# Where the first norm's root is applied: to x ahead of the in-projection, or to what the in-projection gives

## The chip, the cores and the metric

One core of one Trainium2 chip. The time is the device time of one launch in microseconds (us), median of the runs shown. The engines of the core are TensorE (PE, with its weight loads PEld), VectorE (DVE), ScalarE (ACT), GpSimd (POOL) and SyncE (SP), which here only issues transfers. Each works through its own queue in order and waits on semaphores.

## The reference, cut to what matters

One layer of a streaming encoder over 512 tokens of width 1024: a first norm, an in-projection whose columns feed a forgetting attention, an mLSTM with a causal convolution, and gates, then cross-attention and an MLP. The part at stake:

```python
xf = x.astype(float32)
xn = (xf * rsqrt(mean(xf * xf, -1) + EPS)) * norm_mix
proj = xn @ w_in
fq, fk, fv, ff, mqk, mv, mo, mi, mf, gpre = split(proj)
y_fox = fox_attention(fq, fk, fv, ff + b_fox_f)
qk = silu(causal_conv(mqk, conv_w, conv_b))
hm = mlstm_chunkwise(mq, mk, mv, mi + b_mlstm_i, mf + b_mlstm_f)
y_ml = norm(hm) * mlstm_norm * sigmoid(mo)
g = sigmoid(gpre + b_gate)
merged = g_fox * (y_fox @ w_up_fox) + g_ml * (y_ml @ w_up_mlstm)
```

The root of a token is one number, so it may be applied before the product or after it.

## The kernel before, in words

Every large product is made of three matmuls: both operands are split into a high part, rounded to the fast format, and a low part, and high*high, high*low and low*high are summed in a bank of PSUM. Four token tiles of 128 are turned on PE so that the contraction lies on the partitions.

**Order.** `make_steps` writes out one list of steps, and every engine walks the same list and does its part of each step. Its backbone are the halves (L132): a half is four contraction slabs of 128 for one output group, 12 matmuls of 512 columns (L1504). A unit of 512 output columns has four groups, so eight halves. `before(h, ...)` puts steps ahead of half h and `after(h, ...)` behind it. Behind a half come first the steps called soon (L351), then the weight splits of the second kind and the `take` of a finished group, then the rest, and last the weight splits of the first kind (L371). The units of `w_in` come in the order fox_v (halves 0 to 7), fox_q (8 to 15), fox_k (16 to 23), conv_q, conv_k (24 to 39), ml_v, ml_o (40 to 55), gate_fox0, gate_ml0, gate_fox1 (56 to 79) and, after two products of the up-projection, gate_ml1.

**Weights.** SP loads `stage` in lots of four slabs (1 MB, L690), into two buffers for `w_in`. A lot is loaded when DVE has made the low parts of the lot that held its buffer (L684). A pair of slabs is split by `split_weights`: ACT writes `w_hi` with the norm's gain as scale (L814), DVE writes `w_lo` (L1093). Pairs 4 and 5 are the lot of halves 8, 10, 12 and 14 (lot 2); pairs 8 and 9 (lot 4) take lot 2's buffer, and their splits stand behind half 8. The ring of split slabs holds 12.

**First norm.** For tile n: ACT squares x with a sum (`norm`, L892) and gives the seed of the root (L902); DVE works out the root (L1072 to L1074) and writes `scaled` = x times root in two pieces (L1278); PE turns eight blocks (`norm_turn`, L1548); ACT writes `act_hi` (two copies, L956) and DVE `act_lo` (L1321) (`norm_split`). PE opens with six warm-up matmuls, turns the gains, and makes nine more warm-up matmuls (L1720); each is two records in the trace.

**What takes the groups.** fox_v and ml_v: a copy on ACT. fox_q and fox_k: ACT writes the high part from the bank (L825), DVE the low part from the bank (L1169, L1173). conv_q and conv_k: ACT copies the bank to `conv_u` (L838) and writes `conv_acc` from the bank (L842), and in the same step DVE adds three shifted terms (L1180); tanh and the product follow one and two halves later. ml_o and the gates: a tanh on ACT from the bank (L845, L855). A bank is free for the group after next once it is taken.

**Attention beside it.** From half 23 on each second half is followed by the forgetting attention of one pair of heads and one tile: `pair_scores` on PE (L1602), in `pair_exp` the maxima on DVE (L1367) and two exponentials on ACT (L990), `pair_norm` on DVE (L1375) one half later. `pair_scores` t waits for the exponentials of t-1. From half 60 the mLSTM tasks stand so, one per half: `scores` t on PE (L1646) waits for the weighted product of t-1 on DVE (L1398). `fox_split` p takes a finished pair (ACT L1028, DVE L1403).

Of the kernel before, what the change touches and what calls it, by code (L numbers as in the profile page):

```python
# [38 lines left out]
WARM_UP = (6, 9)  # L39
# [177 lines left out]
def make_steps():  # L217
# [10 lines left out]
    def first(name):  # L228
# [115 lines left out]
    for i, (n, j, c, *_) in enumerate(HALVES):  # L344
        b, a = at.pop(i, ([], []))
        steps += b + [("half", i)]
        if in_products(n):
# [3 lines left out]
        soon = [x for x in a if x[0] in ("pair_exp", "pair_norm", "pair_turned", "probs", "turned", "conv_tanh",  # L351
                                      "conv_silu", "split_weights")]
# [34 lines left out]
    for step, n in steps:  # L387
        spread.append((step, n))
        if step == "norm" and n != 1:
            spread += [("norm_root", n), ("norm_scale", n)]  # L390
# [3 lines left out]
def trunk(nc, x, mem, norm_mix, norm_xattn, norm_mem, norm_mlp, w_in, b_fox_f, b_mlstm_i, b_mlstm_f,  # L394
# [6 lines left out]
    with ExitStack() as ctx:  # L401
# [27 lines left out]
        stat = sb("stat", [P, 2, 8])  # L429
        first_sum, first_mean = sb("first_sum", [P, NT]), sb("first_mean", [P, NT])  # L430
# [37 lines left out]
        dwt = at("dwt", 56, [P, TOK])  # L468
        conv_u = at("conv_u", 58, [P, 2, TOK + 16])
# [51 lines left out]
        s_xroot = sem("s_xroot")  # L521
# [23 lines left out]
        s_qhigh = sem("s_qhigh")  # L545
# [164 lines left out]
        def _(pool):  # L710
# [60 lines left out]

            pool.wait_ge(s_value, X0)
# [12 lines left out]
            pool.wait_ge(s_scaled, 2 * (NT + 2))  # L785
            load_row(row_b, norm_xattn, s_row_b)
            load_row(row_a, norm_mlp, s_row_a)
            pool.wait_ge(s_scaled, 2 * (2 * NT + 2))
# [4 lines left out]
        def _(act):  # L793
# [23 lines left out]
            def take(g):  # L817
# [6 lines left out]
                if k == "fox_q":  # L824
                    act.activation(fq_hi[:, j, :], b[:], ACT.Copy, scale=FOX_HD ** -0.5).then_inc(s_qhigh, 1)  # L825
                elif k == "fox_k":
                    copy(fk_hi[:, j, :], b[:]).then_inc(s_qhigh, 1)
                elif k == "fox_v":
                    copy(fox_v[:, j, :], b[:]).then_inc(free, 1)
                elif k == "ml_v":  # L830
                    copy(ml_v[:, j, :], b[:]).then_inc(free, 1)
                elif k in ("conv_q", "conv_k"):
                    c = j + (4 if k == "conv_k" else 0)
                    if c == 0:
                        act.wait_ge(s_const, N_CONST)
                    if c >= 2:
                        act.wait_ge(s_acc, c - 1)
# [950 lines left out]
```

## Time and profile before

| | us |
|---|---|
| median of 3 runs (935.67 to 935.85) | 935.72 |
| the profiled execution | 935.99 |
| its span on the core | 934.3 |
| TensorE busy | 921.0 |
| VectorE busy | 551.6 |
| ScalarE busy | 427.6 |

The span is what the trace covers; the execution's own time is 1.7 us longer. Matmuls are pipelined: a record of 512 columns is shown as 0.39 us, while the next one starts 0.23 us after it. The page gives the granted clock of PE as a share of full speed, and the column reads 1.00 ahead of its first event.

### The profile page before, as it was taken

The page shows a single profiled execution, that of the slowest core. Times are in us where ns is not written, and L with a number is a line of the kernel's source. Part 1 is how long each engine was busy: PE and PEld are TensorE (multiplying, and loading weights), DVE is VectorE, ACT ScalarE, POOL GpSimd, SP SyncE. Part 2 cuts the span into 40 slices and gives each one's busy share as a digit, 9 for nine tenths or more (in the row PEclk, how much of TensorE's full clock was granted, in tenths as well). Part 3 has the DMA queues.
Part 4 walks back from the last instruction along what each step waited for, and adds up shares of the span by engine and source line. Part 5 has one row for each costly group of instructions (what it writes and reads, how often), then busy time and mean ns, then how long its engine had stood idle before and what let it go on. Part 6 is the DMA issues. An engine that isn't in the chain of part 4 may idle for free.

```text
span 934.3 us, 11910 instructions
## 1 busy us (share of the span) xinstructions
PE 921.0 (99%) x4614; PEld 758.3 (81%) x4614; DVE 551.6 (59%) x997; ACT 427.6 (46%) x744; POOL 15.5 (2%) x40
## 2 busy tenths in 40 slices
PE   7999999999999999999999999999999999999997
PEld 6878778777787888889888778988888888888886
DVE  5534777424557645778143545668847956885543
ACT  5544466534433314345244543376346436534523
POOL 5000000000000000000000000000000000000000
PEclk9999999999999999999999999999999999999999
DMA  7311222122201552344421432120621261062202
GB/s 274 130 35 62 90 91 69 42 71 91 90 1 46 188 173 90 112 136 133 161 91 45 136 135 91 46 90 1 225 91 46 90 226 46 1 226 90 90 1 91
DMA packets 44687, 92.10 MB, mean 99 GB/s; under 512 B 1764, under 2 KB 1864, under 8 KB 44632
## 3 DMA queue, kind: packets, MB, share of 16 engines
q1 hardware_dynamic: 43048, 86.02, 27.3%
q0 software_dynamic: 1568, 5.32, 1.6%
q8 instruction: 37, 0.61, 0.3%
q14 instruction: 18, 0.15, 0.1%
q10 hardware_dynamic: 16, 0.00, 0.0%
HBM read 89.24 MB, written 2.10 MB: 98 GB/s over the span
## 4 chain that ended last, share of the span: by engine, by line
PE 87%; DVE 7%; ACT 4%; issue 1%; ACTq 0%; POOL 0%; DVEq 0%; POOLq 0%
PE bank L1504 64%; PE bank L1535 12%; DVE w_lo L1093 2%; DVE conv_acc L1180 2%; PE bank L1660 1%; PE bank L1709 1%; ACT w_hi L795 1%; PE bank L1548 1%; PE bank L1646 1%; PE bank L1687 1%; PE bank L1674 1%; DVE peak L1367 1%; PE bank L1602 1%; PE bank L1629 1%; PE bank L1614 0%
## 5 line engine op out<-in xcount | busy, mean ns | idle before, releaser
L1504 PE MATMUL bank<-act_hi,w_hi 128*128 128x512 f32 (+1 forms) x640 | 247.7, 387 | 0.1
L1504 PE MATMUL bank<-act_hi,w_lo 128*128 128x512 f32 (+1 forms) x640 | 242.8, 379 | 0.0
L1504 PE MATMUL bank<-act_lo,w_hi 128*128 128x512 f32 (+1 forms) x640 | 242.4, 379 | 0.0
L1089 DVE TENSOR_TENSOR w_lo<-stage,w_hi 128x1024 fp32r<-128x1024 f32 x130 | 153.0, 1220 | 65.0 <-ACT w_hi L795 64.6
L795 ACT ACTIVATE w_hi<-stage 128x1024 fp32r<-128x1024 f32 x130 | 130.3, 1051 | 89.7 <-PE bank L1504 31.7
L1504 PEld LDWEIGHTS bank<-act_hi,w_lo 128*128 128x128 f32 x640 | 120.3, 188 | 23.1
L1504 PEld LDWEIGHTS bank<-act_hi,w_hi 128*128 128x128 f32 x640 | 120.6, 188 | 22.2 <-DVE w_lo L1089 0.6
L1504 PEld LDWEIGHTS bank<-act_lo,w_hi 128*128 128x128 f32 x640 | 120.6, 188 | 21.3
L1504 PE MATMUL bank<-w_hi,act_hi 128*128 128x512 f32 (+1 forms) x264 | 102.9, 390 | 3.8 <-DVE act_lo L1321 2.0
L1504 PE MATMUL bank<-w_hi,act_lo 128*128 128x512 f32 (+1 forms) x264 | 101.2, 383 | 0.0
L1504 PE MATMUL bank<-w_lo,act_hi 128*128 128x512 f32 (+1 forms) x264 | 101.1, 383 | 0.0
L1093 DVE SCALAR_TENSOR_TENSOR w_lo<-stage,gain_col,w_hi 128x512 fp32r<-128x512 f32 x88 | 60.3, 746 | 26.3 <-ACT w_hi L795 26.3
L1504 PEld LDWEIGHTS bank<-w_hi,act_hi 128*128 128x128 f32 x264 | 49.6, 188 | 14.5 <-issue 2.8
L1504 PEld LDWEIGHTS bank<-w_hi,act_lo 128*128 128x128 f32 x264 | 49.6, 188 | 9.8
L795 ACT ACTIVATE w_hi<-stage,gain_col 128x512 fp32r<-128x512 f32 x88 | 56.2, 713 | 2.5 <-PE bank L1504 2.5
L1504 PEld LDWEIGHTS bank<-w_lo,act_hi 128*128 128x128 f32 x264 | 49.7, 188 | 9.4 <-issue 0.2
L1221 DVE TENSOR_TENSOR act_lo<-ff,act_hi 128x512 fp32r<-128x512 f32 (+1 forms) x32 | 18.9, 592 | 60.2 <-ACT act_hi L795 60.0
L865 ACT ACTIVATE ff<-bank 128x512 f32<-128x512 f32 x32 | 19.0, 593 | 49.1 <-PE bank L1504 49.1
L1535 PE MATMUL bank<-w_hi,act_hi 128*128 128x512 f32 x96 | 37.3, 389 | 0.0
L1535 PE MATMUL bank<-w_lo,act_hi 128*128 128x512 f32 x96 | 37.3, 389 | 0.0
L1535 PE MATMUL bank<-w_hi,ff_lo 128*128 128x512 f32 x96 | 37.3, 389 | 0.0
L795 ACT ACTIVATE act_hi<-bank 128x512 fp32r<-128x512 f32 x32 | 17.6, 596 | 35.4 <-PE bank L1548 30.0
(290 smaller groups left out, 1292.9 us busy)
## 6 DMA issues: line engine op xcount, KB each, us to landing
stage<-in_w_in SPq DMA_DIRECT2D x20, 1024.0 KB, 5.0
stage<-in_w_mlp_in SPq DMA_DIRECT2D x16, 1024.0 KB, 5.3
stage<-in_w_mlp_out SPq DMA_DIRECT2D x16, 1024.0 KB, 5.5
stage<-in_w_xkv SPq DMA_DIRECT2D x8, 1024.0 KB, 4.9
stage<-in_w_mix_out SPq DMA_DIRECT2D x4, 1024.0 KB, 4.9
stage<-in_w_xq SPq DMA_DIRECT2D x4, 1024.0 KB, 5.7
stage<-in_w_xo SPq DMA_DIRECT2D x4, 1024.0 KB, 4.9
x_tok<-in_x SPq DMA_DIRECT2D x4, 512.0 KB, 7.3
```

Of the source, the lines that this page charges most:

```text
L795: return act.activation(dst, src, ACT.Copy, **k)
L865: act.activation(ff[:, t, :], b[:], ACT.Relu).then_inc(free, 1)
L1089: dve.tensor_tensor(w_lo[:, r:r + 2, :], stage_pair(pair), w_hi[:, r:r + 2, :].bitcast(F32), ALU.subtract).then_inc(s_low, 1)
L1093: ins = dve.scalar_tensor_tensor(w_lo[:, r + d, :], stage_pair(pair)[:, d, :], gain_of(pair, d), w_hi[:, r + d, :].bitcast(F32), ALU.mult, ...
L1180: ins = dve.scalar_tensor_tensor(acc, u[:, q:q + TOK], conv_taps[:, c, q:q + 1], acc, ALU.mult, ALU.add)
L1221: dve.tensor_tensor(act2_lo[:, t, toks], ff[:, t, toks], act2_hi[:, t, toks].bitcast(F32), ALU.subtract).then_inc(s_al, 1)
L1367: dve.tensor_reduce(peak[:], two[1][:, :, 0:P * (n % NT + 1)], AX_X, ALU.max, negate=True)\
L1504: ins = pe.matmul(dst, still[q], moving[q], start=(k == 0 and q == 0), stop=(k == nk - 1 and q == 2))
L1535: ins = pe.matmul(dst, s, w[:, slab % RING, :], start=(u == 0 and g == 0), stop=(u == 3 and g == 2))
L1548: ins = pe.transpose(bank[2 + 2 * (n % 2) + b][:, P * q:P * q + P], scaled[:, n % 2, P * k:P * k + P], ident[:])
L1602: pe.matmul(bank[2 + d][:, 0:keys], still, moving, start=(q == 0), stop=False)
L1629: ins = pe.matmul(bank[6 + p % 2][r:r + FOX_HD, P * i:P * i + P], fox_v[:, j, col:col + FOX_HD], prob_t[:, d, P * j:P * j + P], start=(j = ...
```

## The change

The roots leave the path of x. PE turns x itself, and the four roots of a tile (`x_root`, one column per token tile) are worked out later. What is laid out by tokens (fox_v, ml_v) gets its root as the scale of ACT's copy. What is laid out by columns needs a row of roots: DVE makes four diagonal matrices from the identity, PE multiplies ones by them into bank 7, and ACT copies the bank to `row_root`; POOL copies that later to `row_root_late`. DVE then multiplies each group of fox_q, fox_k, conv_q, conv_k, ml_o and the gates out of its bank by the row, and ACT works from what DVE wrote. The low parts of fox_q and fox_k and the sums of the convolution become steps of their own, one half later; tanh and product of the convolution move by one half too. The nine warm-up matmuls become one. The order of the first steps changes.

```diff
-WARM_UP = (6, 9)
+WARM_UP = (6, 1)
...
-    steps += [("norm", 0), ("split_weights", 0), ("norm_turn", 0), ("norm_split", 0), ("split_weights", 1),
-              ("split_weights", 2), ("norm", 1), ("split_weights", 3), ("norm_root", 1), ("norm_scale", 1)]
-    after(1, ("norm_turn", 1), ("norm_split", 1), ("norm", 2))
-    after(2, ("norm_turn", 2), ("norm_split", 2), ("norm", 3))
-    after(4, ("norm_turn", 3), ("norm_split", 3), ("split_weights", 4), ("split_weights", 5))
+    steps += [("norm_turn", 0), ("norm_split", 0), ("split_weights", 0), ("split_weights", 1)]
+    before(1, ("norm_turn", 1), ("norm_split", 1), ("split_weights", 2), ("split_weights", 3), ("norm", 0),
+           ("norm_root", 0))
+    before(3, ("norm_turn", 2), ("norm_split", 2), ("norm", 1), ("norm_root", 1))
+    before(5, ("norm_turn", 3), ("norm_split", 3), ("norm", 2), ("norm_root", 2))
+    after(5, ("norm", 3), ("norm_root", 3), ("split_weights", 4), ("split_weights", 5))
+    before(first("fox_q") + 1, ("spread_roots", 0))
+    for p in range(2 * PAIRS):
+        after(group_end(UNIT["fox_q" if p < PAIRS else "fox_k"], p % PAIRS), ("fox_low", p))
...
-        after(g + 1, ("conv_tanh", c))
-        after(g + 2, ("conv_silu", c))
+        after(g + 1, ("conv_sum", c))
+        after(g + 2, ("conv_tanh", c))
+        after(g + 3, ("conv_silu", c))
...
+            pool.wait_ge(s_row_root, 1)
+            pool.wait_ge(s_fturn, N_FOX)
+            pool.tensor_copy(row_root_late[:], row_root[:]).then_inc(s_row_late, 1)
...
                 if k == "fox_q":
-                    act.activation(fq_hi[:, j, :], b[:], ACT.Copy, scale=FOX_HD ** -0.5).then_inc(s_qhigh, 1)
+                    taken(act, g)
+                    copy(fq_hi[:, j, :], fq_scaled[:, j, :]).then_inc(s_qhigh, 1)
...
                 elif k == "fox_v":
-                    copy(fox_v[:, j, :], b[:]).then_inc(free, 1)
+                    act.wait_ge(s_xroot, j + 1)
+                    copy(fox_v[:, j, :], b[:], scale=x_root[:, j:j + 1]).then_inc(free, 1)
...
-                    copy(conv_u[:, c % 2, 3:3 + TOK], b[:]).then_inc(s_conv_u, 1)
+                    taken(act, g)
                     if c >= 2:
                         act.wait_ge(s_silu, c - 1)
                     act.wait_ge(s_prep, 1)
-                    act.activation(conv_acc[:, c % 2, :], b[:], ACT.Identity, scale=conv_taps[:, c, 3:4],
-                                   bias=conv_bias[:, c:c + 1]).then_inc(free, 1)
+                    act.activation(conv_acc[:, c % 2, :], conv_u[:, c % 2, 3:3 + TOK], ACT.Identity,
+                                   scale=conv_taps[:, c, 3:4], bias=conv_bias[:, c:c + 1]).then_inc(s_conv_u, 1)
...
+                elif step == "spread_roots":
+                    act.wait_ge(s_spread, 1)
+                    copy(row_root[:], bank[7][:]).then_inc(s_row_root, 1)
...
                 if k == "fox_q":
-                    dve.wait_ge(s_qhigh, j + 1)
-                    dve.scalar_tensor_tensor(fq_lo[:, j, :], b[:], FOX_HD ** -0.5, fq_hi[:, j, :].bitcast(F32),
-                                             ALU.mult, ALU.subtract).then_inc(free, 1)
+                    group_done(dve, g)
+                    dve.wait_ge(s_row_root, 1)
+                    dve.scalar_tensor_tensor(fq_scaled[:, j, :], b[:], FOX_HD ** -0.5, row_root[:],
+                                             ALU.mult, ALU.mult).then_inc(free, 1)
...
+                    dve.tensor_tensor(conv_u[:, c % 2, 3:3 + TOK], b[:], row_root[:], ALU.mult).then_inc(free, 1)
+                elif k == "ml_o":
+                    group_done(dve, g)
+                    dve.tensor_tensor(ml_th[:, j, :], b[:], row_root[:], ALU.mult).then_inc(free, 1)
+                elif k in ("gate_fox", "gate_ml"):
...
+                    group_done(dve, g)
+                    dve.wait_ge(s_row_late, 1)
+                    dve.tensor_tensor(dst, b[:], row_root_late[:], ALU.mult).then_inc(free, 1)
...
-                if n < NT:
-                    for c in (slice(0, HALF_W), slice(HALF_W, DM)):
-                        dve.tensor_scalar(scaled[:, n % 2, c], x_tok[:, n, c], st[:, 2:3], None, ALU.mult)\
-                           .then_inc(s_scaled, 1)
-                    return
...
+                elif step == "spread_roots":
+                    for i in range(NT):
+                        dve.tensor_scalar(root_diag[:, P * i:P * i + P], ident[:], x_root[:, i:i + 1], None, ALU.mult)\
+                           .then_inc(s_diag, 1)
...
+                if n < NT:
+                    pe.wait_ge(s_xt[n], 16)
...
+                elif step == "spread_roots":
+                    for i in range(NT):
+                        pe.wait_ge(s_diag, i + 1)
+                        ins = pe.matmul(bank[7][:, P * i:P * i + P], ones[:], root_diag[:, P * i:P * i + P],
+                                        start=True, stop=True)
+                    ins.then_inc(s_spread, 1)
```

## Rows read from the trace of the kernel before

**Rows 1.** The page: part 1, busy time; part 4, the chain's shares by engine.

```profile
PE 921.0 (99%) x4614; PEld 758.3 (81%) x4614; DVE 551.6 (59%) x997; ACT 427.6 (46%) x744; POOL 15.5 (2%) x40
...
PE 87%; DVE 7%; ACT 4%; issue 1%; ACTq 0%; POOL 0%; DVEq 0%; POOLq 0%
```

**Rows 2.** Waits of PE: line and releaser, us in total, times, longest us.

```profile
PE bank L1504 <- DVE act_lo L1321: 2.0, 2, 1.0
PE bank L1646 <- DVE ml_den L1398: 2.0, 3, 1.3
PE bank L1504 <- DVE w_lo L1093: 1.8, 2, 0.9
```

**Rows 3.** Windows: length, busy time and instructions of each engine, clock, DMA.

```profile
88.00:162.00 74.00, 74.00 (x451) 58.91 (x449) 53.27 (x94) 45.44 (x98) 0.00 (x0) 1.00 0.23 73
...
223.00:292.00 69.00, 66.90 (x350) 52.76 (x347) 39.73 (x127) 26.92 (x53) 0.00 (x0) 1.00 0.15 47
```

**Rows 4.** Timeline, first 20 us: start, us, engine, line, operation, [idle before <-releaser].

```profile
4.21 1.06 ACT L892 ACTIVATE scaled<-x_tok 128x1024 f32<-128x1024 f32 x1 [1.30 <-DMA x_tok<-in_x]
...
4.71 1.70 PE L1721 MATMUL bank<-ones 128*128 128x128 f32 x7
...
5.46 0.29 ACT L902 ACTIVATE stat<-stat,eps 128x1 f32<-128x1 f32 x1
...
5.66 1.32 ACT L795 ACTIVATE w_hi<-stage,gain_col 128x512 fp32r<-128x512 f32 x2
...
6.63 1.22 PE L1721 MATMUL bank<-ones 128*128 128x128 f32 x7
...
7.42 1.41 DVE L1093 SCALAR_TENSOR_TENSOR w_lo<-stage,gain_col,w_hi 128x512 fp32r<-128x512 f32 x2
...
7.69 1.04 PE L1548 MATMUL bank<-ident,scaled 128*128 128x128 f32 x8
...
8.32 1.08 ACT L795 ACTIVATE act_hi<-bank 128x512 fp32r<-128x512 f32 x2 [1.35 <-PE bank L1548]
8.95 1.29 DVE L1321 TENSOR_TENSOR act_lo<-bank,act_hi 128x512 fp32r<-128x512 f32 x2
...
9.70 0.50 PE L1504 MATMUL bank<-w_hi,act_hi 128*128 128x512 f32 x1 [0.98 <-DVE act_lo L1321]
...
19.63 0.50 PE L1504 MATMUL bank<-w_hi,act_hi 128*128 128x512 f32 x1 [1.02 <-DVE act_lo L1321]
```

**Rows 5.** The chain of waits in order of time, the piece of halves 5 to 9.

```profile
29.86 13.61 PE bank L1504 x60
```

**Rows 6.** Timeline of DVE and ACT, 28 to 94 us.

```profile
28.15 2.74 DVE L1093 SCALAR_TENSOR_TENSOR w_lo<-stage,gain_col,w_hi 128x512 fp32r<-128x512 f32 x4 [0.89 <-ACT w_hi L795]
...
38.56 2.55 ACT L795 ACTIVATE w_hi<-stage,gain_col 128x512 fp32r<-128x512 f32 x4
...
39.92 2.74 DVE L1093 SCALAR_TENSOR_TENSOR w_lo<-stage,gain_col,w_hi 128x512 fp32r<-128x512 f32 x4 [0.40 <-ACT w_hi L795]
...
93.49 0.48 DVE L1375 TENSOR_SCALAR prob<-prob,inv 128x128 f32<-128x128 f32 x2
```

**Rows 7.** The page, part 6: transfers by line, KB each, us from issue to landing.

```profile
stage<-in_w_in SPq DMA_DIRECT2D x20, 1024.0 KB, 5.0
```

**Rows 8.** Timeline of DVE, ACT and PE, 84 to 163 us.

```profile
84.69 0.69 DVE L1173 TENSOR_TENSOR fk_lo<-bank,fk_hi 128x512 fp32r<-128x512 f32 x1 [0.58 <-ACT fk_hi L795]
...
137.47 2.32 DVE L1180 SCALAR_TENSOR_TENSOR conv_acc<-conv_u,param,conv_acc 128x512 f32<-128x512 f32 x3 [1.86 <-ACT conv_acc L842]
139.71 0.68 DVE L1403 TENSOR_TENSOR yf_lo<-bank,yf_hi 128x512 fp32r<-128x512 f32 x1
...
160.38 0.68 DVE L1367 TENSOR_REDUCE peak<-bank 128x2 f32<-128x512 f32 x1
...
161.09 0.47 ACT L990 ACTIVATE prob_b<-bank,peak 128x256 f32<-128x256 f32 x1 [1.27 <-DVE peak L1367]
...
162.17 0.45 PE L1602 MATMUL bank<-fk_hi,fq_hi 64*128 64x384 f32 x2
```

More of the change, by code:

```diff
@@ L388, in make_steps @@
         spread.append((step, n))
-        if step == "norm" and n != 1:
+        if step == "norm" and n >= NT:
             spread += [("norm_root", n), ("norm_scale", n)]
@@ L1171, in take @@
                 elif k == "fox_k":
-                    dve.wait_ge(s_qhigh, PAIRS + j + 1)
-                    dve.tensor_tensor(fk_lo[:, j, :], b[:], fk_hi[:, j, :].bitcast(F32), ALU.subtract)\
-                       .then_inc(free, 1)
+                    group_done(dve, g)
+                    dve.tensor_tensor(fk_scaled[:, j, :], b[:], row_root[:], ALU.mult).then_inc(free, 1)
                 elif k in ("conv_q", "conv_k"):
                     c = j + (4 if k == "conv_k" else 0)
-                    u, acc = conv_u[:, c % 2, :], conv_acc[:, c % 2, :]
@@ L1178, in take @@
-                    taken(dve, g)
-                    for q in range(CONV_K - 1):
-                        ins = dve.scalar_tensor_tensor(acc, u[:, q:q + TOK], conv_taps[:, c, q:q + 1], acc,
-                                                       ALU.mult, ALU.add)
-                        if q < CONV_K - 2:
-                            link(ins)
-                    ins.then_inc(s_acc, 1)
+                    group_done(dve, g)
+                    if c == 0:
+                        dve.wait_ge(s_const, N_CONST)
@@ new lines, in take @@
+                    if c >= 2:
+                        dve.wait_ge(s_acc, c - 1)
+                    dve.tensor_tensor(conv_u[:, c % 2, 3:3 + TOK], b[:], row_root[:], ALU.mult).then_inc(free, 1)
+                elif k == "ml_o":
+                    group_done(dve, g)
+                    dve.tensor_tensor(ml_th[:, j, :], b[:], row_root[:], ALU.mult).then_inc(free, 1)
+                elif k in ("gate_fox", "gate_ml"):
+                    t = 4 * order(n) + j
+                    dst = gate_f[:, t, :] if k == "gate_fox" else gate_m[:, j, :]
+                    if k == "gate_ml" and order(n) == 1:
+                        dve.wait_ge(s_merged, 4)
+                    if k == "gate_ml" and order(n) == 0:
+                        dve.wait_ge(s_silu, 2 * 4)
+                    group_done(dve, g)
+                    dve.wait_ge(s_row_late, 1)
+                    dve.tensor_tensor(dst, b[:], row_root_late[:], ALU.mult).then_inc(free, 1)
@@ L1222, in take, with fox_low, conv_sum @@
                                       ALU.subtract).then_inc(s_al, 1)
+            def fox_low(p):
+                value, high, low = (v[:, p % PAIRS, :] for v in ((fq_scaled, fq_hi, fq_lo) if p < PAIRS else
+                                                                 (fk_scaled, fk_hi, fk_lo)))
+                dve.wait_ge(s_qhigh, p + 1)
+                dve.tensor_tensor(low, value, high.bitcast(F32), ALU.subtract).then_inc(s_qlow, 1)
+            def conv_sum(c):
+                u, acc = conv_u[:, c % 2, :], conv_acc[:, c % 2, :]
+                dve.wait_ge(s_conv_u, c + 1)
+                for q in range(CONV_K - 1):
+                    ins = dve.scalar_tensor_tensor(acc, u[:, q:q + TOK], conv_taps[:, c, q:q + 1], acc,
+                                                   ALU.mult, ALU.add)
+                    if q < CONV_K - 2:
+                        link(ins)
+                ins.then_inc(s_acc, 1)
             def silu(c):
@@ L1335, in _ @@
                     dve.wait_ge(s_gturn, 1)
-                    b16 = bias16[:].unsqueeze(1).to_broadcast([P, NT, 16])
-                    link(dve.tensor_tensor(gate16[:], bank[7][:, 0:16 * NT].rearrange("p (i g) -> p i g", g=16),
-                                           b16, ALU.add))
+                    for i in range(NT):
+                        link(dve.scalar_tensor_tensor(gate16[:, i, :], bank[7][:, 16 * i:16 * i + 16],
+                                                      x_root[:, i:i + 1], bias16[:], ALU.mult, ALU.add))
                     f = gate16[:, :, 0:rows]
@@ L1593, in pair_scores @@
                 if i == 0:
-                    taken(pe, GROUP0[UNIT["fox_k"]] + p)
+                    pe.wait_ge(s_qlow, PAIRS + p + 1)
                 if t >= 1:
```

75 lines of the change are left out of this document (45 added, 30 removed).

## The prediction, made blind

> **What bounds the kernel now.** The page comes first: PE is busy 921.0 of 934.3 us and holds 87% of the chain [rows 1]. So a gain must come from stretches where PE waits, and a loss comes from making it wait. The waits of PE show where those are [rows 2]: twice about 1.0 for `act_lo` and twice 0.9 for `w_lo`, all in the opening, and three waits in the mLSTM stage, 2.0 together. Nothing else holds PE. The windows show how thin its cover is: between 88 and 162 us, convolution beside attention, DVE is busy 53.3 of 74 us, between 223 and 292 us it is busy 39.7 of 69 [rows 3]. The timeline of the opening is what the change rebuilds [rows 4]; the chain piece gives PE's pace, 13.61 / 60 = 0.227 us per matmul, so 2.73 per half, and places half 9 at about 40.6 [rows 5].
>
> **Opening.** Removed: square, seed and roots (ACT 1.06 + 0.29) and two scalings per tile ahead of the turn. x has landed at 4.2, when ACT starts on it. Before, the first turn began at 7.69; now PE is through its gains and one warm-up (two records) at about 4.55 and turns at once, 3.1 us earlier. What then follows, by the new order:
> - Clock. Seven warm-up records from 4.71 take 0.213 each; of the seven from 6.63 to the turn at 7.69 about three take 0.213 and four 0.107 [rows 4]. So PE was at 1.2 GHz until about 7.2 and at 2.4 GHz after it, and the eight turns at 2.4 GHz started about 0.11 apart. At 4.55 they go at the slow pace: four blocks by about 5.6, eight by 6.5.
> - ACT: `act_hi` 5.65 and 6.53 (0.54 each), then w_hi of pair 0 to 8.35, of pair 1 to 9.65. DVE: w_lo of pair 0 (1.41, 1.37 within a run) from 8.4 to 9.8. First matmul at 9.9, against 9.70: the split of pair 0 used to run under the warm-ups and now follows `act_hi` on ACT. Nothing is gained.
> - Pair 1's w_lo ends at 11.1, so half 0 is 12 matmuls in a row, to 12.65 at full clock. Only then comes turn 1, and ACT's w_hi of pairs 2 and 3 stands behind `act_hi` of tile 1, which waits for that turn: `act_hi` 13.35 to 14.4 (0.63 after the turn as in [rows 4]), w_hi 14.4 to 16.95, w_lo from 15.7 to 18.4, half 1's last six matmuls 18.6 to 20.0. Half 2 starts at 20.0 against 19.63: +0.35.
> - The clock was not up when PE fell idle at 6.5. It was up after the warm-ups had run without a gap from 4.12 to 7.2, and half 0 has no such run ahead of it. Bounds: half 0 at 2.4 GHz costs nothing; all 12 matmuls at 1.2 GHz cost 12 x 0.227 = 2.7. I take 2.0, near the slow end, since every record before 7.2 is slow and the rise may fall inside half 0. Opening: +2.35, between -0.5 (turns fast too) and +3.05.
> The Trainium skill, page TensorE: Matmul & The Clock Gate, section Part 4: PE-mode transpose, says that turns don't count as activity for the clock as matmuls do; that speaks against trading warm-ups for turns, and by it the 2.7 is nearer than nothing. The trace before neither bears it out nor denies it, since its turns came after the rise.
>
> **Row of roots, ahead of half 9.** New: four DVE scalings of 128x128 (0.20 to 0.28 each, 0.88 together by the row of two in 0.48 [rows 6]), eight PE records of 0.11 (0.9), an ACT copy of 0.6. On DVE they stand behind the w_lo of pairs 8 and 9, whose splits close the steps of half 8. Before, ACT began these at 38.56 and DVE at 39.92, to 42.66 [rows 6], while PE ran half 9 from 40.6: this was covered, and now PE must wait for it. It also gets later. The splits of pairs 4 and 5 move from behind half 4 to behind half 5, so on ACT behind `act_hi` of tile 3 (29.5 to 30.6) and the square and seed of tile 2 (to 31.9). w_hi runs to 34.45, w_lo ends at 35.95, where it ended at 30.9 [rows 6]. That end lets SP load lot 4. Landing takes 5.0 [rows 7] (4.7 here): 40.65 in place of 35.6. Then w_hi 40.7 to 43.25, w_lo 42.0 to 44.75, diagonals to 45.65, the last two records of PE, half 9 at 45.95. Against 40.6: **+5.35**, of which PE works 0.9. Low bound 0.9 (diagonals in time), high bound with a half run at 1.2 GHz behind the pause: +2.7. Both times move with the opening.
>
> **Multiplications.** 36 on DVE (8 fox, 8 convolution, 4 ml_o, 16 gates), by `fk_lo` 0.69 each or 0.60 in a run [rows 8]: 22 us of DVE, less eight scalings. ACT loses eight copies. fox_q, fox_k: one group per 5.5 us, covered; `fox_low` one half later is long ahead of the scores. A bank is now freed by one DVE instruction, which costs nothing while DVE comes within a group's time. Gates' roots by tile, POOL's copy: covered (DVE idle around 62 us; a half lies between the last pair turn and the first use).
> - Attention, 88 to 162. A convolution tile now needs mult, ACT's `conv_acc`, three sums (2.32 [rows 8]) in two halves, and DVE's maxima queue behind the sums of the step before. I walked the order half by half. First split burst: scores lose about 0.1 at 99.5; second (half 31): exponentials 0.45 late, slack 0.9, covered. At half 35 `yf_lo`, which ran at 139.7 behind the sums [rows 8], comes ahead of them and waits for ACT's `yf_hi` behind exponentials, tanh and `conv_acc`: DVE stands 2.3 us, the maxima of half 37 come 1.5 late (slack 1.1 to the next scores after the ACT part: covered). The lateness doesn't heal before the burst of halves 39 and 40, where two w_lo of 2.74 enclose mult and sums. The maxima at 160.38 come at 162.0, the exponentials end at 163.7 in place of 162.1, and the scores at 162.17 had no slack [rows 8]: +1.6. Together **+1.7**; bounds 0 and 2.9 (all multiplications of the burst uncovered, 1.2 more).
> - mLSTM, 223 to 292. PE's three waits for `ml_den` [rows 2] say that DVE is the last link there. In the steps with a `take` the multiplication stands ahead of the next task's work on DVE, and ACT's tanh then behind it. Where the half's end frees DVE early it runs under PE's values, turns and scores. Three places have no slack: ahead of task 1 (0.6), behind the weight bursts of halves 63/64 (0.7) and 71 (0.9: 0.6 and a tanh ahead of the exponential). **+2.2**, bounds 0 and 2.9.
>
> **Sum.** 2.35 + 5.35 + 1.7 + 2.2 = 11.6. The profiled execution took 935.99 (span 934.3 and 1.7 around it) and would take 947.6; it stood 0.27 above the median, so against the runs: 935.72 + 11.6 = 947.3.
>
> **Rivals.**
> - Faster. The opening's 3.1 us arrive: half 2 starts at 16.5, and the row of roots costs its 0.9 of PE work alone. For it: PE waits 3.8 us there now. Against it: the order of ACT above. Time 935.7 - 3.1 + 0.9 = 933.5. It decides at the first matmul of half 2: later than 19.63 - 0.9 = 18.7 there is no gain left, even with all else covered. 4%.
> - The clock falls in the pauses. PE stands about 3.6 us twice in the opening and over 4 before half 9. If half 9 starts at 1.2 GHz, +2.7, and a second half as much: 950.0 to 952.7. The trace before has no pause over 1.2 us after its rise, so it bears neither. 15%. The Trainium skill, page TensorE: Matmul & The Clock Gate, section HAM oscillation, describes such falls behind waits for data; no run here shows it yet.
> - Lot 4 and the diagonals come in time: the row costs 0.9, time 942.9. 12%.
> - The late maxima and multiplications are covered after all: 947.3 - 3.9 = 943.4. 20%.
> - All parts are covered but the row's 0.9, or they cancel: within 0.2%, which is about what a measurement of this kernel can tell from no change (1.9 us). 4%.
> - The forecast: 45%.
>
> **Numbers.** Slower 0.45 + 0.15 + 0.12 + 0.20 = 0.92, same 0.04, faster 0.04. Range: from the forecast without attention and mLSTM, with a good opening (5.35 - 0.5 = 4.9: 940.6) to the forecast with the high opening and half 9 slow (11.6 + 0.7 + 2.7: 950.7): 940.5 to 951.
>
> **What would show it.** First turn near 4.6 but first matmul near 9.9; w_hi of pair 2 near 14.4 or later; half 2 at 20 to 22; a wait of PE for the diagonals or `w_lo` over 3 us before half 9, with lot 4 landing about 5 us after the w_lo of pair 5; a wait of `pair_scores` of 1 to 2 us once; waits for `ml_den` near 4 us in place of 2.0; a granted clock of 0.5 in the first windows. Wrong if PE reaches half 9 with the diagonals there, or if half 2 starts before 18.7.

## The result, and the profile after

The changed kernel takes **953.09 us** (median of 4 runs, 952.38 to 954.61) beside 935.79 for the kernel before on the same chip (4 runs, 935.67 to 936.3): ratio 1.0186, 95% interval 1.0173 to 1.0199. It is slower, as forecast, but by 17.3 us and not by 11.6; the time lies 2.1 us over the upper end of the range. The profiled execution took 952.66 with a span of 950.3, beside 935.99 and 934.3, so 16.0 of its 16.7 us lie in the span.

The page, parts 1 and 2: busy time, and the granted clock in 40 slices of 23.8 us.

```profile
PE 925.9 (97%) x4606; PEld 761.7 (80%) x4606; DVE 573.0 (60%) x1032; ACT 425.8 (45%) x737; POOL 15.1 (2%) x41
...
PEclk9989999999999999999999999999999999999999
```

DVE's busy time rose by 21.4 against [rows 1], which is about what 36 multiplications and the four diagonals, less eight scalings, should give. PE's rose by 4.9 with eight records fewer: PE had no more to do, it did it more slowly. The waits of PE (line and releaser, us in total, times, longest):

```profile
PE bank L1555 <- DVE w_lo L1111: 6.9, 2, 3.5
PE bank L1786 <- DVE root_diag L1376: 4.9, 1, 4.9
PE bank L1701 <- DVE ml_den L1448: 3.3, 4, 1.3
...
PE bank L1657 <- ACT prob_b L1006: 0.9, 2, 0.7
PE bank L1729 <- ACT prob_t L810: 0.8, 1, 0.8
```

Against [rows 2] there are three long pauses: two of 3.5 for `w_lo`, where the longest wait of the opening was 1.0, and one of 4.9 for the diagonals of the roots. `ml_den` is at 3.3 in place of 2.0. The scores wait 0.7 (`prob_b`), and once the turns of the next weights (`ident`, `prob`) wait 0.8 for ACT's copy of the last ones to `prob_t`, which stands behind a gate's tanh.

Where did the 16.0 us come from? The sharpest view is a subtraction: the start of the first matmul of each half in both traces, and where their difference jumps.

```
half    before    after     later by   step
0         9.70    10.08       0.38    +0.38
1        13.69    19.17       5.47    +5.10
2        19.63    23.17       3.54    -1.93
3        23.28    27.12       3.84    +0.30   opening: 3.84
9        40.59    51.19      10.60    +6.76
10       43.60    55.97      12.37    +1.77   row of roots: 8.53
27      100.54   113.16      12.62    +0.25
43      163.16   176.41      13.25    +0.63   attention: 0.88
61      231.21   245.26      14.06    +0.81
65      247.89   262.27      14.38    +0.33
66      253.19   268.20      15.01    +0.63
73      284.75   300.76      16.00    +0.99   mLSTM: 2.75
last                         16.03
```

**The opening** after, by the timelines of PE, ACT and DVE (start, us, engine, line, operation, [idle before <-releaser]):

```profile
4.72 1.91 PE L1603 MATMUL bank<-ident,x_tok 128*128 128x128 f32 x8
...
7.16 2.55 ACT L810 ACTIVATE w_hi<-stage,gain_col 128x512 fp32r<-128x512 f32 x4
...
8.52 2.74 DVE L1111 SCALAR_TENSOR_TENSOR w_lo<-stage,gain_col,w_hi 128x512 fp32r<-128x512 f32 x4 [0.53 <-ACT w_hi L810]
...
10.08 0.77 PE L1555 MATMUL bank<-w_hi,act_hi 128*128 128x512 f32 x1 [3.45 <-DVE w_lo L1111]
...
14.40 0.39 PE L1555 MATMUL bank<-w_hi,act_lo 128*128 128x512 f32 x1
14.64 1.03 PE L1603 MATMUL bank<-ident,x_tok 128*128 128x128 f32 x8
...
16.24 2.55 ACT L810 ACTIVATE w_hi<-stage,gain_col 128x512 fp32r<-128x512 f32 x4
...
17.61 2.74 DVE L1111 SCALAR_TENSOR_TENSOR w_lo<-stage,gain_col,w_hi 128x512 fp32r<-128x512 f32 x4 [0.42 <-ACT w_hi L810]
...
19.17 0.47 PE L1555 MATMUL bank<-w_hi,act_hi 128*128 128x512 f32 x1 [3.50 <-DVE w_lo L1111]
```

The turn at 4.72 and the first matmul at 10.08 (9.9 forecast) are where the walk of the queues had put them. The first turn's eight blocks take 1.91 where the second's take 1.03, and half 0 takes 4.56, from 10.08 to the next turn at 14.64, where 12 matmuls at 0.227 need 2.73 [rows 5]: it is slow by 1.8. Pair 2's `w_hi`, which waits on ACT for turn 1, starts at 16.24 in place of 14.4, late by as much. The record of the granted clock says the same: it rises at 13.8, is back at half speed from 20.6 to 24.0 and again from 47.9 to 54.7. Windows in and behind those stretches (length, busy time of PE, PEld, DVE, ACT, POOL with counts, clock, DMA share, GB/s):

```profile
20.70:23.90 3.20, 3.20 (x9) 2.55 (x8) 0.32 (x2) 0.49 (x1) 0.00 (x0) 0.50 0.70 209
...
48.00:54.00 6.00, 4.54 (x15) 3.96 (x16) 1.99 (x6) 0.60 (x1) 0.00 (x0) 0.50 0.66 225
56.00:60.00 4.00, 4.00 (x19) 3.31 (x19) 2.02 (x6) 0.63 (x1) 0.00 (x0) 1.00 0.00 0
```

**The row of roots**, the timelines of ACT, DVE and PE from 37 to 56 us:

```profile
45.10 2.56 ACT L810 ACTIVATE w_hi<-stage,gain_col 128x512 fp32r<-128x512 f32 x4 [1.80 <-DMA stage<-in_w_in]
...
37.14 2.74 DVE L1111 SCALAR_TENSOR_TENSOR w_lo<-stage,gain_col,w_hi 128x512 fp32r<-128x512 f32 x4 [0.61 <-ACT w_hi L810]
...
46.47 2.74 DVE L1111 SCALAR_TENSOR_TENSOR w_lo<-stage,gain_col,w_hi 128x512 fp32r<-128x512 f32 x4 [2.12 <-ACT w_hi L810]
49.12 0.87 DVE L1376 TENSOR_SCALAR root_diag<-ident,x_root 128x128 f32<-128x128 f32 x4
...
49.46 2.08 PE L1786 MATMUL bank<-root_diag,ones 128*128 128x128 f32 x8 [4.87 <-DVE root_diag L1376]
51.19 0.77 PE L1555 MATMUL bank<-act_hi,w_hi 128*128 128x512 f32 x1
51.76 0.63 PE L1555 MATMUL bank<-act_lo,w_hi 128*128 128x512 f32 x1
```

Read it as a chain: `w_lo` of pairs 4 and 5 ends at 39.88 and frees the buffer, lot 4 is there at 45.10 (5.2 later; 5.0 in [rows 7]), ACT has waited 1.8 for it, `w_lo` of pairs 8 and 9 ends at 49.1, only then come the four scalings of 0.87 together, and PE has stood 4.9. Its eight records are 1.73 from first start to half 9, in place of 0.9, and half 9 begins with matmuls of 0.43 start to start instead of 0.23.

**Attention and mLSTM**, DVE, ACT and PE (150 to 176 us, then 258 to 260):

```profile
150.38 0.69 DVE L1453 TENSOR_TENSOR yf_lo<-bank,yf_hi 128x512 fp32r<-128x512 f32 x1 [2.23 <-ACT yf_hi L810]
151.84 0.68 DVE L1273 SCALAR_TENSOR_TENSOR ml_k<-conv_th,conv_acc 128x512 f32<-128x512 f32 x1
152.44 2.32 DVE L1263 SCALAR_TENSOR_TENSOR conv_acc<-conv_u,param,conv_acc 128x512 f32<-128x512 f32 x3
154.68 1.22 DVE L1417 TENSOR_REDUCE peak<-bank 128x2 f32<-128x1024 f32 x1
...
161.25 0.42 DVE L1417 TENSOR_REDUCE peak<-bank 128x2 f32<-128x256 f32 x1
164.29 2.74 DVE L1111 SCALAR_TENSOR_TENSOR w_lo<-stage,gain_col,w_hi 128x512 fp32r<-128x512 f32 x4 [2.62 <-ACT w_hi L810]
...
173.63 0.69 DVE L1417 TENSOR_REDUCE peak<-bank 128x2 f32<-128x512 f32 x1
...
175.42 0.44 PE L1657 MATMUL bank<-fk_hi,fq_hi 64*128 64x384 f32 x2 [0.68 <-ACT prob_b L1006]
...
258.45 0.68 DVE L1213 TENSOR_TENSOR gate_f<-bank,row_root_late 128x512 f32<-128x512 f32 x1
259.05 0.41 DVE L1439 TENSOR_REDUCE ml_m<-bank 128x1 f32<-128x256 f32 x1
259.21 0.72 ACT L867 ACTIVATE gate_f<-gate_f,param 128x512 f32<-128x512 f32 x1 [2.23 <-issue]
260.32 0.46 ACT L1022 ACTIVATE dwt<-bank,ml_m 128x256 f32<-128x256 f32 x1
```

DVE does stand 2.2 us for `yf_hi` (2.3 forecast). The maxima that stood at 160.38 [rows 8] stand at 173.63; taking off the 12.62 that PE had already lost, they are 0.63 late, and the scores wait 0.68. In the mLSTM stage the multiplication delays the maximum by 0.60, and the tanh that it lets go on ACT (0.72) stands ahead of the exponential.

### The profile page after: what moved, and what is told of

It reads as the page before. It is cut to its first block, busy times and chain, and to the rows that moved or that the text cites. A ratio compares the mean times of both kernels' runs of the same rounds, so it can differ in the third digit from the quotient of the medians.

```text
span 950.3 us, 11977 instructions
## 1 busy us (share of the span) xinstructions
PE 925.9 (97%) x4606; PEld 761.7 (80%) x4606; DVE 573.0 (60%) x1032; ACT 425.8 (45%) x737; POOL 15.1 (2%) x41
## 4 chain that ended last, share of the span: by engine, by line
PE 69%; DVE 1%; ACT 1%; issue 1%; ACTq 0%; DVEq 0%
PE bank L1555 51%; PE bank L1586 12%; PE bank L1715 1%; PE bank L1764 1%; PE bank L1603 1%; PE bank L1729 1%; PE bank L1742 1%; PE bank L1701 1%; ACT w_hi L810 0%; DVE w_lo L1111 0%; ACT dwt L1022 0%; PE bank L1749 0%; ACT ff L879 0%; DVE w_lo L1107 0%; PE bank L1702 0%
## 5 line engine op out<-in xcount | busy, mean ns | idle before, releaser
L1555 PEld LDWEIGHTS bank<-act_lo,w_hi 128*128 128x128 f32 x640 | 121.0, 189 | 21.4
L1555 PEld LDWEIGHTS bank<-w_hi,act_hi 128*128 128x128 f32 x264 | 50.4, 191 | 17.3 <-issue 7.8
L1555 PEld LDWEIGHTS bank<-w_hi,act_lo 128*128 128x128 f32 x264 | 50.5, 191 | 10.1
```

The costliest lines, as they stand in the source:

```text
L1555: ins = pe.matmul(dst, still[q], moving[q], start=(k == 0 and q == 0), stop=(k == nk - 1 and q == 2))
```

## The experiments

Two theories went in. **A: queues.** The time follows from the order of work on ACT and DVE, the clock adds some 2 us. **B: clock.** The granted clock is low at each of the three pauses and behind it, and that makes up the part that the forecast lacks. Times are medians beside the kernel before in the same batch (935.81 to 936.07). "Later by" is the same subtraction as in the table above.

### Keep PE busy in all three pauses: keep_clock

```diff
+                    for _ in range((9, 15, 0, 0)[n] if n < NT else 0):
+                        pe.matmul(bank[7][:, 0:P], ones[:], ones[:], start=True, stop=True)
                 elif step == "spread_roots":
+                    for _ in range(20):
+                        pe.matmul(bank[7][:, 0:P], ones[:], ones[:], start=True, stop=True)
```

> The changed kernel with idle work for TensorE in its three pauses: 9 products of ones behind the first turn, 15 behind the second, 20 ahead of the row of roots. The queues' order is as changed. If the clock is what my forecast missed, all pauses stay and the granted clock stays at 2.4 GHz from the first half on: about 947.5 us, 5.5 below the changed kernel, and half 9 starts some 5 to 6 us late instead of 6.8 plus 1.8 behind it. Rival (the excess is queueing on VectorE, not the clock): less than 1 us is won, 952 to 953.

Measured 945.95 (945.76 to 946.57), ratio 1.011 [1.0093, 1.0127]: 7.1 below the changed kernel, with work added. The clock is high from 4.8 us until past the last matmul. PE's timeline:

```profile
4.71 1.08 PE L1603 MATMUL bank<-ident,x_tok 128*128 128x128 f32 x8
5.62 2.17 PE L1784 MATMUL bank<-ones 128*128 128x128 f32 x18
...
9.29 0.47 PE L1555 MATMUL bank<-w_hi,act_hi 128*128 128x512 f32 x1 [1.49 <-DVE w_lo L1111]
...
45.12 1.16 PE L1790 MATMUL bank<-root_diag,ones 128*128 128x128 f32 x8 [0.18 <-DVE root_diag L1376]
46.03 0.48 PE L1555 MATMUL bank<-act_hi,w_hi 128*128 128x512 f32 x1
```

The eight turns take 1.08 and not 1.91, the records of the roots 1.16 and not 2.08. The fast turns aren't the edit's doing: the products stand behind them, and the clock rose at 4.8, before the first product. So up to 0.8 us of the gain can be the moment of that rise, which differs between executions (last section). Half 2 starts at 19.48, 0.14 earlier than in the kernel before; between halves 3 and 9 another 5.72 are lost, and 0.11 in half 9; attention costs 0.88 and mLSTM 2.76. This is the change with the clock kept high, 10.1 us, and the clock's part is 7.1 of 17.3. Theory A alone is out: the clock cost more than the 5.8 of the row of diagonals.

### The pauses one at a time: keep_opening, keep_row

The same edit with (9, 15) in the opening alone, or with the 20 products ahead of the row alone.

> The changed kernel with 9 and 15 products of ones behind the first two turns alone. If the opening's slow stretches cost what the shift of half 3 says (3.8 us with them, -0.1 in the kernel with all pauses filled), this kernel takes 949 us, 4 below the changed one, and with the kernel above the two effects add up to the 7.1 of the kernel with all three pauses filled. Rival (the row has most of it): 951 or more.

> The changed kernel with 20 products of ones ahead of the row of roots alone. If the fall of the clock behind half 8 costs what the trace of the changed kernel shows there (records of the row 0.21 in place of 0.11 us: 0.9; half 9 and what follows 1.8; less 0.3 for products that outlast the wait), this kernel takes 950.6 us, 2.5 below the changed one. Rival (the fall there costs less than a microsecond and the opening has it all): 952 or more.

keep_opening: 947.69 (947.54 to 948.2), 5.4 below the changed kernel. keep_row: 951.19 (949.7 to 951.91), 1.9 below. Together 7.3, beside 7.1 for both at once: within the scatter of these runs (2.2 us in keep_row) the parts add up. (In single traces the opening's part is 4.0 and not 5.4, since its slow stretches fall differently from execution to execution; see the last section.) In the trace of keep_row half 9 is later by 5.77 more than half 8 and no slow half follows; in that of keep_opening it is 6.39 and half 10 is later by another 1.32. The larger share is the opening's, where the changed kernel has two slow stretches (up to 13.8, and from 20.6 to 24.0).

### The row of roots ahead of the weight splits: row_first

```diff
-    before(first("fox_q") + 1, ("spread_roots", 0))
+    after(first("fox_q"), ("spread_roots", 0))
```

> The changed kernel with one step moved: the row of roots stands ahead of the splits of pairs 8 and 9, which close the steps of half 8, instead of behind them. If the pause of 5.0 us and the slow half behind it come from that place in VectorE's queue, half 9 starts about 1.1 us later than before the change relative to half 8 instead of 6.8, and the clock doesn't fall there: 945.7 us. Rival (the diagonals are late anyway, because the roots are late): 951 or more.

Measured 945.49, ratio 1.0103 [1.0088, 1.0118]; 945.7 was expected. The timelines of DVE and PE:

```profile
42.29 2.74 DVE L1111 SCALAR_TENSOR_TENSOR w_lo<-stage,gain_col,w_hi 128x512 fp32r<-128x512 f32 x4 [0.62 <-ACT w_hi L810]
44.95 0.87 DVE L1376 TENSOR_SCALAR root_diag<-ident,x_root 128x128 f32<-128x128 f32 x4
...
45.28 1.16 PE L1786 MATMUL bank<-root_diag,ones 128*128 128x128 f32 x8
46.20 0.48 PE L1555 MATMUL bank<-act_hi,w_hi 128*128 128x512 f32 x1
```

The same four scalings now end while PE still has work, PE does not wait, and half 9 is later by 1.06 and half 10 by 0.12, in place of 6.76 + 1.77. The clock stays up there: its last low stretch ends at 24.5. Of the 8.5 us of the row, 7.4 were its place in the queue and the low clock that came with the wait; the row itself is PE's 0.9 and little more.

### The splits of pairs 4 and 5 back behind half 4: splits_back

```diff
-    after(5, ("norm", 3), ("norm_root", 3), ("split_weights", 4), ("split_weights", 5))
+    after(4, ("split_weights", 4), ("split_weights", 5))
+    after(5, ("norm", 3), ("norm_root", 3))
```

> The changed kernel with the splits of pairs 4 and 5 back behind half 4, where they stood before. If the late landing of lot 4 makes half of the pause, w_lo of pair 5 ends about 5 us earlier, the splits of pairs 8 and 9 no longer wait for the transfer, the pause falls from 5.0 to about 2.5 us and the clock stays up: 948 us. Rival (only the order behind half 8 counts): the pause stays near 5 us, 952 to 953.

Measured 949.25 (948.22 to 951.17), ratio 1.0146 [1.013, 1.0161]: 1.3 over the 948 expected. Lot 4 is there when ACT wants it, and the wait for the diagonals falls from 4.9 to 2.3 (waits of PE; window at the start of half 9):

```profile
PE bank L1787 <- DVE root_diag L1377: 2.3, 1, 2.3
```

```profile
48.50:51.80 3.30, 3.30 (x11) 2.62 (x10) 0.00 (x0) 0.60 (x1) 0.00 (x0) 0.50 0.98 330
```

Half 9 is later by 3.41 and half 10 by another 1.63. So 2.6 of the row's wait was the late lot of weights, as expected; that the clock would stay up was wrong, it fell behind a pause half as long too, and the 1.63 of half 9's slow matmuls is about the size of the miss.

### Pairs 2 and 3 ahead of tile 1's turn: open_order

```diff
-    steps += [("norm_turn", 0), ("norm_split", 0), ("split_weights", 0), ("split_weights", 1)]
-    before(1, ("norm_turn", 1), ("norm_split", 1), ("split_weights", 2), ("split_weights", 3), ("norm", 0),
+    steps += [("norm_turn", 0), ("norm_split", 0), ("split_weights", 0), ("split_weights", 1),
+              ("split_weights", 2), ("split_weights", 3)]
+    before(1, ("norm_turn", 1), ("norm_split", 1), ("norm", 0),
```

> The changed kernel with the splits of pairs 2 and 3 ahead of tile 1's turn and split. If ScalarE's order in the opening is what holds half 1, half 1 follows turn 1 without a pause and half 2 starts at about 18.3 us instead of 23.2 (19.6 before the change): 948 us. Rival (the opening is bound by the landing of the weights or by the slow clock alone): half 2 at 21 or later, 951 or more.

Measured 947.21, ratio 1.012 [1.0105, 1.0136]. Half 2 starts at 18.30, as expected. PE goes from the turn into the matmuls without a pause:

```profile
14.69 1.04 PE L1604 MATMUL bank<-ident,x_tok 128*128 128x128 f32 x8
15.49 0.48 PE L1556 MATMUL bank<-w_hi,act_hi 128*128 128x512 f32 x1
```

The second pause of the opening was therefore the order alone: weights that had landed stood on ACT behind an activation that waits for PE. Without that pause the fall of the clock at 20.6 did not come either: it rises at 13.9 and next falls at 44.6, at the row of roots.

### Leave the multiplications out: gates_free, conv_free

gates_free leaves out the gates' 16 multiplications, conv_free the convolution's eight (ACT then reads the bank, as before).

```diff
-                    dve.wait_ge(s_row_late, 1)
-                    dve.tensor_tensor(dst, b[:], row_root_late[:], ALU.mult).then_inc(free, 1)
...
-                    act.activation(dst, dst, ACT.Tanh, scale=0.5, bias=gate_bias[:, col:col + 1]).then_inc(s_tgate, 1)
+                    act.activation(dst, b[:], ACT.Tanh, scale=0.5, bias=gate_bias[:, col:col + 1]).then_inc(free, 1)
```

> The changed kernel with the 16 multiplications of the gates left out, and their tanh taken by ScalarE from the bank as before the change (the gates' root is left out of the computation). If these multiplications on VectorE make the mLSTM stage's loss, the shift of TensorE's halves grows by nothing between halves 61 and 73 instead of 2.8 us: 950.3 us. Rival (the stage is late for another reason, such as the order of the steps or POOL's copy): 952.5 or more.

> The changed kernel with the 8 multiplications of the convolution's groups left out: ScalarE copies the bank and writes conv_acc from it as before the change (the roots are left out of the convolution's inputs); the sums, tanh and product stay one half later. If the multiplication makes the attention stage's loss of 1.0 us, it goes: 952.1. Rival (the later sums, which stand between the maxima and the weights' bursts, make it): the shift at halves 27 and 43 stays, 953.

gates_free: 949.82 (948.94 to 951.91), ratio 1.0152 [1.0138, 1.0166]. Behind half 43 nothing is lost any more (later by 12.12 there and 12.10 at the end), and the waits for `ml_den` are back at the 2.0 of [rows 2]:

```profile
PE bank L1694 <- DVE ml_den L1441: 2.0, 3, 1.3
```

All 2.8 us of the mLSTM stage come with the gates' multiplications (the edit also lets ACT's tanh go ahead without waiting for them; gates_order, further down, tells the two apart in part). conv_free: 953.62 (951.82 to 953.79), ratio 1.0185 [1.0171, 1.0199]; its time decides nothing, for the scatter of its runs is larger than what is sought. The trace tells it: half 27 keeps its 0.27, half 43 loses 0.30 in place of 0.63. So about half of that step is the multiplications, the rest is order.

### The three moves together: three_moves

row_first, splits_back and open_order, with nine products of ones behind turn 0.

> The changed kernel with all three moves and nine products of ones behind the first turn: row of roots ahead of the splits of pairs 8 and 9, splits of pairs 4 and 5 behind half 4, splits of pairs 2 and 3 ahead of tile 1. If the single effects add up: opening 1.3 to 3 us earlier than the kernel before, row 1.1, attention 1.0, mLSTM 2.8, so 937.7 to 939.4 us. Rival (each move only uncovers the next wait in the opening): 942 or more.

Measured 937.57 (11 runs, 936.94 to 937.93), ratio 1.0017 [1.0008, 1.0026]: 15.5 of the 17.3 us are back. The clock is high from 6.4 on, half 2 starts at 16.57, which is 3.06 before the kernel before, half 9 loses 0.80 and half 10 another 0.10, attention 0.86, mLSTM 2.72. The 3.1 us that the early turn promised do exist, but they need both: in the old order with the clock kept (keep_clock) half 2 was 0.14 early, in this order without the products of ones (open_order) 1.33. The opening's gain pays for the row and most of the rest; what is left is +1.3 in the span, and attention and mLSTM with their 3.6 are the places to get it from.

### What is left: gates_later, gates_order, fox_late, first_weights

All four start from three_moves. gates_later has both engines take the groups of gate_fox0, gate_ml0 and gate_fox1 one half later; gates_order does so for ACT's tanh, and on DVE for one group alone; fox_late moves `fox_low` 7 by two halves and `fox_split` 0 by one; first_weights splits pair 0 ahead of tile 0.

```diff
 gates_later
+    for unit in ("gate_fox0", "gate_ml0", "gate_fox1"):
+        for j in range(4):
+            after(group_end(UNIT[unit], j), ("gate_take", GROUP0[UNIT[unit]] + j))
...
 fox_late
-        after(pair_at[NT * p + NT - 1] + 6, ("fox_split", p))
+        after(pair_at[NT * p + NT - 1] + (7 if p == 0 else 6), ("fox_split", p))
...
 first_weights
-    steps += [("norm_turn", 0), ("norm_split", 0), ("split_weights", 0), ("split_weights", 1),
+    steps += [("split_weights", 0), ("norm_turn", 0), ("norm_split", 0), ("split_weights", 1),
```

> The kernel of the three moves, with the take of gate_fox0, gate_ml0 and gate_fox1 one half later, behind the next mLSTM task's work on VectorE. If it is their place ahead of that work which costs, 1 to 1.7 of the 2.8 us come back: about 1.3 us below the kernel of the three moves. Rival (VectorE lacks the time wherever they stand): the same within 0.4 us.

Measured 940.26, ratio 1.0048 [1.0036, 1.0061]: a miss, 2.7 worse and not 1.3 better. At half 61 it gains what was hoped for (0.48 gained in place of 0.80 lost), but the places behind it lose 1.9 (half 66), 0.6 (half 71), 1.9 (halves 73 to 75) and 1.6 (half 81). The waits of PE, and a window at halves 73 to 75:

```profile
PE bank L1710 <- DVE ml_den L1457: 4.2, 3, 1.9
...
PE bank L1564 <- DVE gate_f L1220: 1.4, 1, 1.4
```

```profile
291.90:295.10 3.20, 3.20 (x11) 2.14 (x10) 1.23 (x4) 0.69 (x1) 0.00 (x0) 0.50 0.02 5
```

At half 81 a multiplication that was put off holds its bank, and PE wants that bank. At half 66 and ahead of half 74 PE waits 1.8 and 1.9 for `ml_den`, and behind the second of these waits the granted clock fell, from 291.8 to 295.2: part of what was lost there is the clock, in the middle of the kernel and behind a wait of less than 2 us. The wait of 1.8 had no such fall behind it.

> The kernel of the three moves, with ScalarE's tanh of gate_fox0, gate_ml0 and gate_fox1 one half later (VectorE's multiplications stay where they are), and the second group of gate_fox0 one half later on VectorE too, so that the take of the last attention pair no longer stands behind it. If ScalarE's tanh ahead of the exponentials and of that take makes part of the loss, the 0.8 us at half 61 goes (the later gates gained 0.5 there) and some tenths behind the bursts: 1.3 to 2 us below the three moves, 935.6 to 936.3. Rival (the whole loss is VectorE's time): the same within 0.4 us.

Measured 936.49 (11 runs, 935.61 to 937.61), ratio 1.0003 [0.9994, 1.0012]: 1.1 below the three moves, where 1.3 to 2 were expected. With DVE's reads left in time but one, the gain at half 61 stays, and the mLSTM stage costs 1.4 in place of 2.7. So about half of it was the place of ACT's tanh and of that one group in the queues, and not DVE's time.

> The kernel of the three moves, with the low part of the last fox_k group two halves later and the take of the first attention pair one half later, behind the sums. If VectorE's two waits for ScalarE there (2.2 us for yf_hi, some tenths for the high part) make the attention stage's loss, the shift of 0.4 at half 27 and of 0.6 at half 43 goes: 0.9 below the three moves. Rival (VectorE's load alone): the same within 0.3 us.

Measured 936.84, ratio 1.0007 [0.9998, 1.0016]. Half 43 gains 0.16 where it lost 0.57, and `yf_lo` runs behind the sums without a wait (DVE):

```profile
137.11 0.68 DVE L1456 TENSOR_TENSOR yf_lo<-bank,yf_hi 128x512 fp32r<-128x512 f32 x1
```

So the attention's larger step goes when DVE no longer stands 2.2 us for `yf_hi`; half of it also went when the convolution's multiplications were left out (conv_free), so both were needed to make it. The smaller step, 0.28 at half 27, stays although the last `fox_low` was moved too; its cause was not found.

> The kernel of the three moves, with the split of pair 0 ahead of tile 0's split on ScalarE and VectorE and six products of ones instead of nine. If ScalarE's queue sets the first matmul, it starts at about 9.0 instead of 9.4 to 10.0 and half 2 some 0.5 us earlier: 937.1. Rival (the landing of the weights and the slow clock set it): no change.

Measured 937.8, ratio 1.0018 [1.0009, 1.0027]: no gain. PE's first wait is for `act_lo` in place of `w_lo`, and the first matmul at 9.39, 0.63 earlier, moves half 2 by 0.07.

### All moves: all_moves

> All of these together: the sum of the three single effects, 2.7 us below the three moves, so about 934.9, which would be 0.9 below the kernel before the change. Rival (effects overlap): 936 or more.

Measured 935.65 (11 runs, 935.48 to 937.35) beside 936.01, ratio 0.9997 [0.9988, 1.0005]. That is 1.9 below the three moves and not 2.7; the three single effects as measured (1.1, 0.7 and -0.2) sum to 1.6, so the expectation had priced them too high and no overlap shows. The last matmul starts 0.96 earlier than in the kernel before, but the measurement can't tell the two apart. No version was found that is clearly faster than the kernel before.

## Why the prediction came out too low

**The failed step is the clock.** The forecast took 2.0 for it, in half 0 alone, bounded it there by 2.7, and charged nothing behind the later pauses. It cost 7.1 by the medians. The profiled traces of the changed kernel and of keep_clock lie 6.8 apart in the span, and there it can be placed: 2.5 up to the start of half 1 (19.17 and 16.67: 0.8 for slow turns, which the forecast's walk held, and 1.7 in half 0, where it took 2.0), 1.2 in half 1 and 0.4 in half 2 (the fall at 20.6, behind a pause of 3.5), 1.0 ahead of half 9 (0.8 of it in the eight records) and 1.7 in half 9 (the fall at 47.9, in the wait for the diagonals). The last four terms, 4.3 together, were not in the forecast, and they are the miss: in the trace the opening came out 1.5 over its term, the row 3.2 over, attention 0.8 under and mLSTM 0.5 over, 4.4 in all. The other 1.3 between 11.6 and 17.3 lie outside the traced spans: 0.7 in what an execution takes around its span, 0.6 in how the two profiled executions stand to their medians.

The rival "the clock falls in the pauses" named the mechanism and got 15%. Its 950.0 to 952.7 still fell short, since it let two halves be slow behind the row and none behind the opening's second pause; the range's upper end let one be slow. The evidence was thin (the longest wait of the trace before, behind the clock's rise, is 1.3 and not the 1.2 of the prediction), but that was a reason to add a slow half behind every forecast pause to the upper end: one more at 2.7, behind the opening's second pause, would have brought it from 950.7 to 953.4. The Trainium skill, page TensorE: Matmul & The Clock Gate, section HAM oscillation, describes slow matmuls behind waits for data. The two falls here, at 20.6 behind a wait of 3.5 us and at 47.9 in one of 4.9, agree with it; in the first pause, of 3.45, the clock had not risen yet.

**Opening, order.** Right. Half 2 was forecast 0.35 late with slow turns and the clock high behind them; keep_clock, whose turns were fast, shows 0.14 early, and open_order shows that the place of pairs 2 and 3 behind `act_hi` of tile 1 cost the gain.

**Row of roots.** Right: 5.35 forecast, 5.72 in keep_clock, by the chain that the prediction wrote down (late `w_lo`, late lot, splits, then diagonals of 0.88). row_first and splits_back remove one link each. row_first came out as expected (945.49, 945.7 expected); in splits_back the wait shrank as expected, and the time missed by 1.3, with the clock's fall behind it.

**Attention.** 1.7 forecast, 0.9 measured. DVE's stand for `yf_hi` was right (2.3 and 2.23). The mis-sized term is the 1.6 for the late maxima: they come 0.63 late. The step under it that failed is "the lateness doesn't heal": taking off PE's 12.62, the maxima that stood at 141.17 come 0.9 late (154.68), those that stood at 148.30 only 0.3 (161.25), and DVE then stands idle for 2.6 us ahead of the burst. A likely reason, which no run isolates: the product for `ml_k` now stands ahead of the sums (151.84, 152.44) and fills time in which DVE waited for `conv_acc` before (1.86 at 137.47 [rows 8]). The two maxima in the kernel before:

```profile
141.17 1.22 DVE L1367 TENSOR_REDUCE peak<-bank 128x2 f32<-128x1024 f32 x1
...
148.30 0.42 DVE L1367 TENSOR_REDUCE peak<-bank 128x2 f32<-128x256 f32 x1
```

**mLSTM.** Right: 2.2 forecast, 2.75 measured (2.72 to 2.76 in keep_clock and three_moves), 0 in gates_free. The three places of the forecast are the three where time is lost: 0.81, 0.96 (halves 65 and 66) and 0.99, for 0.6, 0.7 and 0.9. Each is a little over its price. That the tanh also delays ACT's copy to `prob_t`, and PE's next turns by 0.8 at 299.05, wasn't foreseen; it falls at the third place, which was priced best, so it doesn't explain the excess at the first two.

**Multiplications.** 0.69 alone, 0.60 in a run, as priced; DVE's 21.4 more busy microseconds cost PE about 3: 2.8 for the gates' (gates_free), 0.3 for the convolution's (conv_free). The rivals with everything covered or with an early opening failed at their own points of decision: half 2 started at 19.48 even with the clock kept, and half 9 waited for the diagonals.

## What to carry to other kernels

A pause of PE can be charged twice: once as the wait, once as matmuls at 1.2 GHz behind it. Here that held for every pause of 2.3 us and more that came when the clock was high, and for one of 1.9; it did not for one of 2.1 (first_weights, ahead of 9.39), one of 1.8 (gates_later) and those of up to 1.6. So each forecast pause needs both terms in the upper end of the range, and a change that takes warm-up work away must say what stands in its place. On queues that run in order, put the short step that PE waits for ahead of weight splits, and put no landed weights behind a step that waits for PE: moves of that kind gave back 7.6 us (row_first) and 5.9 (open_order) of 17.3, each by itself. The scale along the free axis didn't ride on ACT's copy here, as the one per partition did for fox_v and ml_v; it cost a DVE instruction of 0.6 to 0.7 us per group, and that was free only where DVE was not the last link.

## What the runs showed of the hardware that was not expected

- The moment at which the clock first rises is not settled by the program. row_first and splits_back, whose openings are the same as that of the changed kernel, rose at 4.0 and 4.1, fell at 7.4 and 7.5 and were slow through half 0; the changed kernel rose at 13.8, keep_row, with the same opening again, at 6.5, and gates_free and conv_free at 5.7 and 5.9. The slow stretches of the opening lie differently with it.
- The clock fell behind a wait of 2.3 us (splits_back) and once behind one of 1.9 (gates_later, at 291.8), not only behind those of 3.5 and 4.9, and in the changed kernel the fall of 20.6 came 1.4 us after the work had resumed.
- The scatter of the runs goes with the clock: 2.2 us between four runs of the changed kernel, 2.2 in keep_row, 0.8 in keep_clock, 0.6 in the kernel before. Two of the changed kernel's runs had a mean granted clock of 0.994 and took 952.38 and 952.66, the other two had 0.989 and took 953.51 and 954.61. The profiled execution is one of the first two, so its trace shows less of the clock's loss than half of the runs had.
